# Memory branch, branch projections and second output projection as split products, memory handed over transposed

## The chip, the cores and the metric

One core of one Trainium2 chip runs the whole program in one launch. The metric is device time in microseconds (us). Three runs of the kernel before were timed; the number to be predicted is the median of the changed kernel. TensorE (PE in the profile, PEld its weight loads) multiplies matrices into PSUM, VectorE (DVE) and ScalarE (ACT) do elementwise work, GpSimd (POOL) and SyncE (SP) only start DMAs here. All arithmetic is in 32-bit floats.

## The reference

256 tokens of width 1024 pass through two layers of a first kind and then two of a second kind. Cut to what the change touches:

```python
def memory_branch(mq, mem, w_mem_kv):                 # mem: 256 x 1024
    mk, mv = jnp.split(mem @ w_mem_kv, 2, axis=-1)    # 512 wide each, 4 heads of 128
    p = softmax(q @ mk.T * 128 ** -0.5)
    return p @ mv

branches = (pool_branch(u_pool), dsa_branch(q, k, v, iq, ik, iw), memory_branch(mq, mem))
merged = sum(sigmoid(gate_logits[n]) * (branches[n] @ w_br[n]) for n in range(3))   # 512 -> 1024 each
x = layer_norm(DN_ALPHA * x + merged @ w_out)
x = layer_norm(DN_ALPHA * x + moe(x))                 # 16 experts, two per token
```

`pool_branch` takes sliding means, `dsa_branch` attends to 64 keys per query that an index score has picked. The second kind of layer has three attentions side by side (called swa, fox and mls in the kernel), whose results, 1024 wide, go through `w_out_2`; a feed-forward of width 4096 follows.

## The kernel before, in words

**Products.** `product` (from L540) has two forms. If both operands come in two parts, a rounded high part (type fp32r) and the rounded rest, it issues three rounded matmuls: high by rest, rest by high, high by high. Otherwise it issues one f32 matmul, which the profile shows as two instructions. The input projections, gates, `w_out` and the feed-forward were split already. The memory keys and values, the projections of the branches (`w_br`), the second output projection (`w_out_2`) and the experts were not.

**Weights.** Each weight piece is up to 1 MB (128 x 2048) and lies in a ring of 9 slots. A split piece takes two positions of the ring: SP loads the raw piece into the first as soon as that slot is released; ACT rounds it into the second (`round_hi`, L1127), once that slot is released too; then DVE subtracts in place (`round_lo`, L1469). An unsplit piece takes one position. SP loads strictly in the order of the plan (`weight_plan`). In each queue the calls `round_hi(n)` and `round_lo(n)` say at which point of that engine's own order all pieces up to number n are split. Nothing else sets when it happens: every engine works through its instructions in the order in which they are written, and waits on semaphores.

**The mixing layer.** Seven `cut`s make the columns z of the input projection (14 pieces, numbers 0 to 13). Between them stand the index scores, the pool branch and the transposition of the index queries, of memory (`pe_turn(("memT", l), mem_rows, ...)`) and of ik. After the last cut come the index scores of block 1, two key pieces (14, 15), the values (16, 17), two query pieces (18, 19), the transposition of the rotated Q and K, and the memory scores. In those same queues DVE finds the 64 best keys of each query (`top`) and rotates Q and K (`rope_heads`); ACT copies results out of PSUM.
Then follow 24 merges: for each of three branches (pool, memory, dsa) eight column groups `dc`. A merge is a gate product (8 chunks by 256 columns, split), a branch product (4 chunks, unsplit), ACT's sigmoid and DVE's multiplication. Each half of a branch (four merges) uses two gate pieces and one `w_br` piece, five positions of the ring. Between the merges of the first branch the two attentions are worked off: scores, exponentials, shares, transposed probabilities, values. `round_hi` and `round_lo` stand at every fourth merge and ask for the next three pieces; the product with `w_out` ("mixed") follows.

**Banks.** Four PSUM banks serve the large products in turn (`dense`), four the small ones (`loose`). A bank is free again when the engine that reads it has signalled; for the branch outputs that is ACT's copy.

**The second kind of layer.** Six cuts, then the three attentions in one long exchange between PE, ACT and DVE, then "attended" (the product with `w_out_2`, four pieces of 128 x 2048), then the feed-forward.

Of the kernel before, what the change touches and what calls it, by code (L numbers as in the profile page):

```python
# [9 lines left out]
ALU = mybir.AluOpType  # L10
# [3 lines left out]
P = 128  # L14
S = 256
# [102 lines left out]
class Signal:  # L118


    def __init__(self, sem, per_layer):
        self.sem, self.per_layer = sem, per_layer

    def at(self, l, i=0):
        return self.sem, l * self.per_layer + i + 1

    def last(self, l):
        return self.sem, (l + 1) * self.per_layer
# [114 lines left out]
def weight_plan(first_layers, second_layers):  # L243

    plan = []
    for l in range(first_layers):
        for cut in Z_CUTS:
            plan += [(w, True) for w in halves("w_in", (l,), (0, D), cut, "rows")]
        plan += [(w, False) for w in halves("w_mem_kv", (l,), (0, D), (0, BANK), "cols")]
        plan += [(w, False) for w in halves("w_mem_kv", (l,), (0, D), (BANK, 2 * BANK), "rows")]  # L250
        plan += [(w, True) for w in halves("w_in", (l,), (0, D), (C_MQ, C_GATE), "cols")]
        for n in BRANCH_ORDER:
            for a in (0, BANK):
                at = C_GATE + n * D + a
                plan += [(w, True) for w in halves("w_in", (l,), (0, D), (at, at + BANK), "cols")]
                plan.append((block("w_br", (l, n), (0, BRANCH), (a, a + BANK)), False))
# [40 lines left out]
def build_program(nc, t, out, first_layers=DEPTH, second_layers=DEPTH):  # L297
    with ExitStack() as ctx:
# [29 lines left out]
        mkT = sb("mkT", MEM_HEADS, N_MEM)  # L328
        mv = sb("mv", TB, BRANCH)
# [31 lines left out]
        mem_rows = shaped(region[:, TB * C_MQ + 4 * TB * 5 * HD:TB * C_MQ + 4 * TB * 5 * HD + TB * D], TB, D)  # L361
        memT = mergedT
        band = shaped(region[:, band_at:band_at + POOL_GROUPS * TB * S], POOL_GROUPS, TB, S)
# [27 lines left out]
        yT = part(KC, S)  # L391
        swa = dict(turned=part(TB, 10 * HD), probs=part(8, S), probsT=part(8, S), qT=part(4, S), kT=part(2, S))
# [71 lines left out]

        x_in, consts_in, params_in, router_in, positions_in, out_stored = (
# [3 lines left out]
        def landed(s, l, loads):  # L469
# [11 lines left out]
        memT_made, mk_made, mv_made, mq_made = (  # L481
            signal(n, c) for n, c in (("memT_made", 4), ("mk_made", 4), ("mv_made", 2), ("mq_made", 4)))
# [4 lines left out]
            signal(n, c) for n, c in (("dsa_scored", 16), ("dsa_lowered", 2), ("dsa_exped", 16), ("dsa_shared", 2),  # L487
                                      ("dsa_turned", 6), ("dsa_out", 8)))
        mem_scored, mem_lowered, mem_exped, mem_shared, mem_turned, mem_out = (
            signal(n, c) for n, c in (("mem_scored", 8), ("mem_lowered", 2), ("mem_exped", 8), ("mem_shared", 2),  # L490
                                      ("mem_turned", 4), ("mem_out", 8)))
# [15 lines left out]
            signal(n, c) for n, c in (("swa_scored", 16), ("swa_lowered", 2), ("swa_exped", 16), ("sink_exped", 2),  # L507
                                      ("swa_shared", 2), ("swa_turned", 6), ("swa_out", 8)))
# [6 lines left out]
            signal(n, c) for n, c in (("fox_scored", 8), ("fox_lowered", 2), ("fox_exped", 8), ("fox_shared", 2),  # L515
                                      ("fox_turned", 3), ("fox_out", 4)))
# [4 lines left out]
            signal(n, c) for n, c in (("mls_valued", 2), ("mls_summed", 2), ("mls_rooted", 2), ("mls_opened", 2), ("mls_y", 1)))  # L521
        relued, relu_squared, hidden_hi, hidden_lo = (
# [167 lines left out]
        def pe_pool(l, groups):  # L690
            for n in groups:
# [7 lines left out]
                i, free, full = loose.take(("pooled", l, n), pooled.at(l, n))  # L699
# [22 lines left out]
        def pe_mem_values(l, b):  # L722
            for h in range(MEM_HEADS):
                i, free, full = loose.take(("mem_out", l, b, h), mem_out.at(l, b * 4 + h))
# [12 lines left out]

        def pe_merge(l, m, dc):

            n, c = BRANCH_ORDER[m], dc % 4  # L740
            branch_ready = (pooled.last(l), mem_out.last(l), dsa_out.last(l))[m]
            if c == 0:
                held_pieces["gates"] = [ring.next() for _ in range(2)]
                held_pieces["projection"] = ring.next()
            gates, projection = held_pieces["gates"], held_pieces["projection"]
# [3 lines left out]
            pe_cols(("branch", l, m, dc), projection, c * P, [branchT[:, 4 * n:4 * n + 4, :]], weighed.at(l, m * 8 + dc),  # L749
# [4 lines left out]
        def tensor_mix(l):  # L754
# [5 lines left out]
            def key_piece(n):  # L760
                piece = ring.next()
                for j in range(2):
                    h = 2 * n + j
                    pe_cols(("mk", l, h), piece, j * P, [memT], mk_made.at(l, h), memT_made.last(l))
# [15 lines left out]
            pe_turn(("memT", l), mem_rows, D, [memT_made.at(l, n) for n in range(4)], landed(mem_in, l, 1))  # L780
# [9 lines left out]
            pe_index(l, 1, range(0, 4))  # L790
            key_piece(0)
            pe_index(l, 1, range(4, 8))
            key_piece(1)
            pe_rows(("mv", l), [memT], BRANCH, [mv_made.at(l, b) for b in range(TB)], memT_made.last(l))
            query_piece(0)
            query_piece(1)
# [15 lines left out]
                      [dsa_out.at(l, n) for n in range(4)], dsa_turned.at(l, 1))  # L812
# [1489 lines left out]
```

## Time and profile before

| | |
|---|---|
| three runs | 2008.25, 2011.35, 2012.51 us |
| median | 2011.35 us |
| the profiled execution | 2013.33 us |
| its span | 2011.8 us |
| TensorE busy | 1753.5 us (87%) in 9214 matmuls |
| VectorE busy | 774.0 us (38%) |
| ScalarE busy | 642.6 us (32%) |
| mean granted TensorE clock | 0.914 |
| weight traffic | 380.30 MB, 49.4% of 16 DMA engines |

The span is that of one execution taken by the profiler. A row of a timeline gives the start in us, the duration in us, the engine, the line of the kernel, the operation, what is written and read, how many instructions are merged into the row, and in brackets how long the engine had been idle and what it waited for. Most matmuls stand under L538, the helper that issues them, so they are told apart by their operands: `ring_rounded` is a split weight piece, `ring_sb` an unsplit one, `region_sb` the working area. A row with one granted clock is a row of the busy times by stretch.

### The profile page before, as it was taken

Reading aid. Unit: us, or ns where it says so; the run is one execution under the profiler, and the core shown is the slowest. Engines: PE = TensorE matmul, PEld = TensorE weight load, DVE = VectorE, ACT = ScalarE, POOL = GpSimd, SP = SyncE. Lnnn points to the kernel's source line nnn. Section 1 sums busy time; section 2 is a strip of 40 time slices with the busy share of each in tenths; the row PEclk is TensorE's granted clock in tenths of the full one; section 3 lists DMA queues with packets and bytes.
Section 4 is the critical chain, followed back from the end, with each engine's and each line's share of the span. In section 5 each row is a group of like instructions: output and inputs, shape, how many; then the busy total and the mean of one; then the engine's idle time right before and its main releaser. Section 6 shows DMA issues by size and latency. Waiting matters only on the chain.

```text
span 2011.8 us, 22089 instructions
## 1 busy us (share of the span) xinstructions
PE 1753.5 (87%) x9214; PEld 1288.5 (64%) x9214; DVE 774.0 (38%) x1476; ACT 642.6 (32%) x1041; POOL 29.5 (1%) x49
## 2 busy tenths in 40 slices
PE   6998986899997998986899995857899988588999
PEld 5777985444435777985444434844599977447997
DVE  4445343210115545333210015643455545515554
ACT  3326422010004336422011013443344444415442
POOL 4000000000000000000000000000000000000000
PEclk9998998799998998998899997965899998678999
DMA  8332345499995432335499992510255545003552
GB/s 258 138 126 93 147 147 219 176 401 421 421 420 178 153 125 89 147 147 218 173 414 421 421 421 99 197 40 0 84 189 188 178 142 183 1 21 126 189 189 105
DMA packets 57663, 392.67 MB, mean 195 GB/s; under 512 B 7124, under 2 KB 7168, under 8 KB 15696
## 3 DMA queue, kind: packets, MB, share of 16 engines
q1 hardware_dynamic: 54144, 380.30, 49.4%
q0 software_dynamic: 3264, 9.61, 1.4%
q8 instruction: 76, 1.25, 0.3%
q10 hardware_dynamic: 144, 1.24, 0.2%
q14 instruction: 35, 0.29, 0.0%
HBM read 390.07 MB, written 1.05 MB: 194 GB/s over the span
## 4 chain that ended last, share of the span: by engine, by line
PE 79%; DVE 10%; ACT 5%; DMA 4%; issue 2%; SPq 0%; DVEq 0%; ACTq 0%
PE psum L538 76%; DMA ring_sb<-in_weights 4%; PE psum L664 2%; ACT ring_rounded L1127 1%; DVE ring_rounded L1469 1%; PE psum L583 1%; ACT region_sb L1153 1%; DVE x_sb L1580 0%; ACT xT_hi_rounded L1352 0%; DVE x_sb L1578 0%; DVE region_sb L1853 0%; DVE region_sb L1856 0%; DVE small_sb L1849 0%; ACT region_sb L1341 0%; DVE region_sb L1847 0%
## 5 line engine op out<-in xcount | busy, mean ns | idle before, releaser
L538 PE MATMUL psum<-ring_sb,region_sb 128*64 128x512 f32 (+1 forms) x1728 | 427.0, 599 | 14.9 <-ACT region_sb L1341 11.0
L1469 DVE TENSOR_TENSOR ring_rounded<-ring_sb,ring_rounded 128x2048 fp32r<-128x2048 f32 (+4 forms) x152 | 321.5, 2130 | 245.6 <-ACT ring_rounded L1127 245.4
L538 PE MATMUL psum<-xT_hi_rounded,ring_rounded 128*128 128x256 f32 x1920 | 357.9, 288 | 0.0
L1127 ACT ACTIVATE ring_rounded<-ring_sb 128x2048 fp32r<-128x2048 f32 (+4 forms) x152 | 268.1, 1781 | 212.7 <-PE psum L538 149.9
L538 PEld LDWEIGHTS psum<-ring_sb,region_sb 128*64 128x64 f32 (+1 forms) x1728 | 148.2, 144 | 277.5 <-issue 260.1
L538 PE MATMUL psum<-ring_rounded,xT_hi_rounded 128*128 128x384 f32 (+4 forms) x960 | 278.3, 367 | 37.1 <-DVE ring_rounded L1469 18.1
L538 PE MATMUL psum<-xT_lo_rounded,ring_rounded 128*128 128x256 f32 x960 | 285.8, 298 | 27.9 <-DVE ring_rounded L1469 16.8
L538 PEld LDWEIGHTS psum<-xT_hi_rounded,ring_rounded 128*128 128x128 f32 x1920 | 308.3, 197 | 1.8 <-issue 0.5
L538 PEld LDWEIGHTS psum<-ring_rounded,xT_hi_rounded 128*128 128x128 f32 x960 | 184.4, 198 | 61.9 <-issue 39.4
L538 PEld LDWEIGHTS psum<-xT_lo_rounded,ring_rounded 128*128 128x128 f32 x960 | 189.7, 198 | 31.6 <-issue 18.1
L538 PE MATMUL psum<-ring_rounded,region_rounded 128*128 128x512 f32 x768 | 178.7, 392 | 3.0 <-DVE region_rounded L2055 3.0
L538 PE MATMUL psum<-ring_rounded,xT_lo_rounded 128*128 128x384 f32 (+4 forms) x480 | 173.9, 362 | 0.0
L538 PEld LDWEIGHTS psum<-ring_rounded,region_rounded 128*128 128x128 f32 x768 | 144.3, 189 | 33.0 <-DVE region_rounded L2055 3.4
L538 PE MATMUL psum<-region_sb 128*64 128x128 f32 (+4 forms) x608 | 128.2, 416 | 5.3 <-ACT region_sb L1147 4.5
L538 PE MATMUL psum<-region_sb,ring_sb 128*128 128x256 f32 x512 | 119.5, 380 | 0.0
L538 PEld LDWEIGHTS psum<-region_sb 64*128 64x128 f32 (+2 forms) x608 | 70.0, 187 | 57.7 <-issue 45.4
L538 PEld LDWEIGHTS psum<-region_sb,ring_sb 128*128 128x128 f32 x512 | 93.7, 190 | 12.0 <-issue 1.3
L538 PEld LDWEIGHTS psum<-ring_rounded,xT_lo_rounded 128*128 128x128 f32 x480 | 95.4, 199 | 6.3
L1803 DVE TENSOR_TENSOR region_sb<-region_sb,psum 128x512 f32<-128x512 f32 x16 | 11.0, 687 | 220.1 <-ACT region_sb L1334 220.1
L1334 ACT ACTIVATE region_sb<-psum 128x512 f32<-128x512 f32 x16 | 9.6, 597 | 216.5 <-PE psum L538 216.5
L1827 DVE TENSOR_SCALAR region_sb<-psum,slot_gate_sb 128x512 f32<-128x512 f32 x32 | 24.0, 751 | 122.9 <-PE psum L538 122.9
L583 PE MATMUL psum<-consts_sb,region_sb 128*128 128x128 f32 x148 | 28.2, 357 | 46.8 <-DVE region_sb L1856 24.9
(239 smaller groups left out, 1345.1 us busy)
## 6 DMA issues: line engine op xcount, KB each, us to landing
ring_sb<-in_weights SPq DMA_DIRECT2D x324, 1024.0 KB, 7.8
ring_sb<-in_weights SPq DMA_DIRECT2D x24, 768.0 KB, 4.3
ring_sb<-in_weights SPq DMA_DIRECT2D x8, 904.0 KB, 4.5
ring_sb<-in_weights SPq DMA_DIRECT2D x8, 900.0 KB, 4.6
ring_sb<-in_weights SPq DMA_DIRECT2D x8, 584.0 KB, 14.3
region_sb<-in_mem POOLq DMA_DIRECT2D x2, 1024.0 KB, 8.5
region_sb<-in_pool_band POOLq DMA_DIRECT2D x2, 1024.0 KB, 10.0
region_sb<-in_ln_g POOLq DMA_DIRECT2D x4, 512.0 KB, 4.3
```

What stands on the lines that cost most here:

```text
L538: return nc.tensor.matmul(dst, lhsT, rhs, start=first, stop=last, skip_group_check=True)
L583: last = nc.tensor.transpose(psum[:, i, j * S + b * P:j * S + (b + 1) * P], src[:, b, (c + j) * P:(c + j + 1) * P], ident)
L664: last = nc.tensor.transpose(psum[:, i, j * P:(j + 1) * P], scores[:, h, kb * P:(kb + 1) * P], ident)
L1127: nc.scalar.activation(rounded(piece.hi), piece.raw, ACT.Copy).then_inc(hi_made, 1)
L1153: nc.scalar.activation(scores[:, h, 0:keys], scores[:, h, 0:keys], ACT.Exp, bias=minus[:, h:h + 1], scale=scale, accum_out=sums[:, h:h + 1 ...
L1334: nc.scalar.activation(opened[pair % 2], psum[:, i, :], ACT.Sigmoid).then_inc(sig_made.sem, 1)
L1469: nc.vector.tensor_tensor(rounded(piece.raw), piece.raw, reread(piece.hi), ALU.subtract).then_inc(lo_made, 1)
L1803: nc.vector.tensor_tensor(rows, sig, psum[:, i, :], ALU.mult).then_inc(sig_read.sem, 1)
L1827: nc.vector.tensor_scalar(y[:, half * BANK:(half + 1) * BANK], psum[:, i, :], slot_gate[:, pair - 1:pair], None, ALU.mult).then_inc(gated. ...
```

## The change

- The two key and two value pieces, the six `w_br` pieces of a mixing layer and the four `w_out_2` pieces of a second layer are now split. Each takes two ring positions instead of one, and ACT and DVE each get 28 more splits in all (152 become 180).
- Their other operands are split too. ACT writes each branch output rounded, and DVE subtracts it from PSUM to make the rest; the bank is then free after DVE (`branch_lo`, `y_lo`), no longer after ACT. That is 20 small instructions per mixing layer and 13 per second layer.
- Memory comes transposed from the host (`mem_turned`), so its 16 transposes and their four copies per mixing layer go; ACT rounds it (128 x 2048) and DVE makes its rest.
- The query pieces now come before the key pieces: 14, 15 query, 16, 17 keys, 18, 19 values. Within a half of a branch the `w_br` piece comes between the two gate pieces. The calls of `round_hi` and `round_lo` are placed anew, in the merges at the second and fourth of four.
- Some semaphores are shared between the two kinds of layer.

```diff
 def weight_plan
-        plan += [(w, False) for w in halves("w_mem_kv", (l,), (0, D), (0, BANK), "cols")]
-        plan += [(w, False) for w in halves("w_mem_kv", (l,), (0, D), (BANK, 2 * BANK), "rows")]
         plan += [(w, True) for w in halves("w_in", (l,), (0, D), (C_MQ, C_GATE), "cols")]
+        plan += [(w, True) for w in halves("w_mem_kv", (l,), (0, D), (0, BANK), "cols")]
+        plan += [(w, True) for w in halves("w_mem_kv", (l,), (0, D), (BANK, 2 * BANK), "rows")]
-                plan += [(w, True) for w in halves("w_in", (l,), (0, D), (at, at + BANK), "cols")]
-                plan.append((block("w_br", (l, n), (0, BRANCH), (a, a + BANK)), False))
+                gates = halves("w_in", (l,), (0, D), (at, at + BANK), "cols")
+                plan += [(gates[0], True), (block("w_br", (l, n), (0, BRANCH), (a, a + BANK)), True), (gates[1], True)]
...
-            plan += [(w, False) for w in halves("w_out_2", (l,), (0, D), (a, a + BANK), "rows")]
+            plan += [(w, True) for w in halves("w_out_2", (l,), (0, D), (a, a + BANK), "rows")]
 TensorE, tensor_mix
-            pe_turn(("memT", l), mem_rows, D, [memT_made.at(l, n) for n in range(4)], landed(mem_in, l, 1))
...
             pe_index(l, 1, range(0, 4))
+            query_piece(0)
+            pe_index(l, 1, range(4, 8))
+            query_piece(1)
             key_piece(0)
-            pe_index(l, 1, range(4, 8))
             key_piece(1)
-            pe_rows(("mv", l), [memT], BRANCH, [mv_made.at(l, b) for b in range(TB)], memT_made.last(l))
-            query_piece(0)
-            query_piece(1)
+            pe_rows(("mv", l), [mem_hi, memT], BRANCH, [mv_made.at(l, b) for b in range(TB)], mem_split.at(l, 1))
 ScalarE, scalar_mix
             def merge(m, dc):
-                if dc % 4 == 0:
-                    round_hi(first + 20 + m * 6 + dc // 4 * 3 + 6)
+                if dc % 2:
+                    round_hi(first + 20 + m * 6 + dc // 4 * 3 + (4 if dc % 4 == 1 else 5))
...
             cut(6)
+            a.wait_ge(*landed(mem_in, l, 1))
+            nc.scalar.activation(rounded(mem_hi), memT, ACT.Copy).then_inc(mem_split.sem, 1)
             index(1, range(0, 4))
+            query_piece(0)
+            index(1, range(4, 8))
+            round_hi(first + 18)
+            query_piece(1)
             key_piece(0)
-            index(1, range(4, 8))
             key_piece(1)
-            round_hi(first + 20 + 2)
+            round_hi(first + 20)
             for b in range(TB):
...
                 nc.scalar.activation(mv[:, b, :], psum[:, i, :], ACT.Copy).then_inc(mv_made.sem, 1)
-            query_piece(0)
-            query_piece(1)
+            round_hi(first + 22)
 VectorE, vector_mix
+            def lower_mem(b):
+                for h in range(MEM_HEADS):
+                    i, _ = loose.of(("mem_out", l, b, h))
+                    v.wait_ge(*mem_out.at(l, b * 4 + h))
+                    nc.vector.tensor_tensor(rounded(z[:, b, C_IQ + h * P:C_IQ + (h + 1) * P]), psum[:, i, 0:P],
+                                            reread(branchT[:, 8 + h, b * P:(b + 1) * P]), ALU.subtract).then_inc(branch_lo.sem, 1)
...
             index(1, range(0, 4))
+            v.wait_ge(*mem_split.at(l, 0))
+            nc.vector.tensor_tensor(rounded(memT), memT, reread(mem_hi), ALU.subtract).then_inc(mem_split.sem, 1)
             index(1, range(4, 8))
-            round_lo(first + 20 + 2)
+            round_lo(first + 20)
             top(1, range(0, 8))
+            round_lo(first + 22)
...
             dsa_shares(0)
+            lower_mem(0)
             mem_scores(1)
...
             merge(0, 4)
+            lower_dsa(0)
             dsa_scores(1, range(0, 4))
             merge(0, 5)
             dsa_scores(1, range(4, 8))
+            lower_mem(1)
 ScalarE, scalar_second
             nc.scalar.activation(low, low, ACT.Ln, bias=const("one")).then_inc(decay_logged.sem, 1)
+            round_hi(first + 14)
...
+            round_hi(first + 16)
             act_mls_weights(l, 0)
 VectorE, vector_second
             swa_scores(1)
+            round_lo(first + 14)
+            lower_values("swa_out", swa_out, 0, 4, 0)
             mls_gates(0)
...
             fox_scores(1)
+            round_lo(first + 16)
             mls_out(1)
             fox_shares(1)
+            lower_values("fox_out", fox_out, 1, 2, 4)
...
+            nc.vector.tensor_tensor(rounded(y_lower[:, 6:8, :]), psum[:, i, :].rearrange("p (c t) -> p c t", c=2),
+                                    reread(yT[:, 6:8, :]), ALU.subtract).then_inc(y_lo.sem, 1)
```

## Rows read from the trace of the kernel before

**Rows 1.** Waits of PE: engine, line <- releaser: us in total, times, longest.

```profile
PE psum L538 <- DVE ring_rounded L1469: 34.9, 6, 8.4
PE psum L538 <- DVE xT_lo_rounded L1732: 16.1, 2, 8.1
PE psum L538 <- ACT upT_sb L1174: 11.0, 2, 5.5
```

**Rows 2.** Timeline of PE, two merges of the first layer.

```profile
215.83 1.89 PE L538 MATMUL psum<-region_sb,ring_sb 128*128 128x256 f32 x8
...
217.92 0.28 PE L538 MATMUL psum<-xT_lo_rounded,ring_rounded 128*128 128x256 f32 x1
...
220.43 1.89 PE L538 MATMUL psum<-region_sb,ring_sb 128*128 128x256 f32 x8
```

**Rows 3.** Values, "attended" (timeline) and "mixed" (chain, start and us).

```profile
128.21 13.90 PE L538 MATMUL psum<-ring_sb,region_sb 128*128 128x512 f32 x32
...
1398.18 30.14 PE L538 MATMUL psum<-ring_sb,region_sb 128*128 128x512 f32 x64 [0.78 <-ACT region_sb L1133]
...
315.56 24.61 PE psum L538 x96
```

**Rows 4.** Timeline from the last cut to the turned K, first layer.

```profile
111.97 1.13 PE L538 MATMUL psum<-region_sb 64*128 64x256 f32 x8
...
128.41 0.38 ACT L1220 ACTIVATE mkT_sb<-psum 128x256 f32<-128x256 f32 x1 [3.07 <-PE psum L538]
128.69 5.50 ACT L1127 ACTIVATE ring_rounded<-ring_sb 128x2048 fp32r<-128x2048 f32 x3
130.62 8.95 DVE L1469 TENSOR_TENSOR ring_rounded<-ring_sb,ring_rounded 128x2048 fp32r<-128x2048 f32 x4 [7.09 <-ACT ring_rounded L1127]
...
142.14 0.60 ACT L1273 ACTIVATE mv_sb<-psum 128x512 f32<-128x512 f32 x1 [2.84 <-PE psum L538]
...
147.78 0.42 DVE L1489 TENSOR_TENSOR region_sb<-region_sb,pos_cos_sb 128x256 f32<-128x256 f32 x1
...
151.73 0.42 DVE L1495 TENSOR_TENSOR region_sb<-region_sb 128x256 f32<-128x256 f32 x1
...
153.46 1.04 PE L583 MATMUL psum<-consts_sb,region_sb 128*128 128x128 f32 x8
159.07 1.97 PE L583 MATMUL psum<-consts_sb,region_sb 128*128 128x128 f32 x8 [4.58 <-DVE region_sb L1495]
```

**Rows 5.** By stretch: busy of PE, PEld, DVE, ACT, POOL; clock, DMA, GB/s.

```profile
159.00:163.90 4.90, 4.83 (x17) 4.20 (x17) 1.79 (x6) 3.42 (x4) 0.00 (x0) 0.50 0.00 0
...
178.50:181.00 2.50, 2.50 (x13) 2.50 (x12) 0.00 (x0) 2.48 (x7) 0.00 (x0) 0.50 0.30 128
...
296.00:301.00 5.00, 4.92 (x24) 4.93 (x25) 3.50 (x5) 0.39 (x2) 0.00 (x0) 0.54 0.00 0
```

**Rows 6.** Timeline of PE: ik is turned.

```profile
59.82 0.44 PE L583 MATMUL psum<-consts_sb,region_sb 128*128 128x128 f32 x2 [0.43 <-DVE region_sb L1683]
```

**Rows 7.** Timeline of PE between the merges of the first branch.

```profile
177.27 1.61 PE L664 MATMUL psum<-consts_sb,region_sb 128*128 128x128 f32 x8 [2.26 <-DVE region_sb L1508]
...
201.37 2.22 PE L538 MATMUL psum<-region_sb 64*128 64x256 f32 x8 [2.24 <-ACT region_sb L1147]
...
226.75 1.91 PE L664 MATMUL psum<-consts_sb,region_sb 128*128 128x128 f32 x16
```

**Rows 8.** Timeline, last half of the third branch and the output projection.

```profile
293.75 1.91 ACT L1127 ACTIVATE ring_rounded<-ring_sb 128x2048 fp32r<-128x2048 f32 x1 [7.30 <-DMA ring_sb<-in_weights]
296.08 0.58 PE L538 MATMUL psum<-xT_lo_rounded,ring_rounded 128*128 128x256 f32 x1 [5.55 <-ACT upT_sb L1174]
...
310.58 1.91 ACT L1127 ACTIVATE ring_rounded<-ring_sb 128x2048 fp32r<-128x2048 f32 x1 [4.29 <-DMA ring_sb<-in_weights]
```

**Rows 9.** Timeline, attentions of the first layer of the second kind.

```profile
1328.72 2.07 PE L538 MATMUL psum<-upT_sb,consts_sb 8*128 8x128 f32 x8 [4.29 <-ACT region_sb L1147]
...
1387.10 0.42 DVE L2000 TENSOR_TENSOR region_sb<-psum,small_sb 128x256 f32<-128x256 f32 x1 [4.32 <-PE psum L538]
```

More of the change, by code:

```diff
@@ L698, in pe_pool @@
                 last.then_inc(full, 1)
[L699 removed]
+                i, free, full = loose.take(("pooled", l, n), branch_lo.at(l, n))
                 pe.wait_ge(*differ_made.at(l, n))
@@ L736, in build_program, with z_columns @@
         held_pieces = {}
+        def z_columns(at):
+            return z[:, :, at:at + 4 * P].rearrange("p b (c t) -> p c b t", c=4)
+        lower_branch = {0: z_columns(C_POOL), 1: dsa_lo, 2: z_columns(C_IQ)}
         def pe_merge(l, m, dc):
             n, c = BRANCH_ORDER[m], dc % 4
-            branch_ready = (pooled.last(l), mem_out.last(l), dsa_out.last(l))[m]
+            branch_ready = branch_lo.at(l, (3, MEM_LO[1] + 3, DSA_LO[1] + 3)[m])
             if c == 0:
-                held_pieces["gates"] = [ring.next() for _ in range(2)]
+                held_pieces["gates"] = [ring.next()]
                 held_pieces["projection"] = ring.next()
+                held_pieces["gates"].append(ring.next())
             gates, projection = held_pieces["gates"], held_pieces["projection"]
@@ L1386, in cut @@
             def cut(n):
-                round_hi(first + 2 * n + 5)
+                round_hi(first + min(2 * n + 5, 2 * len(Z2_CUTS)))
                 c0, c1 = Z2_CUTS[n]
@@ L1659, in merge @@
             def merge(m, dc):
-                if dc % 4 == 0:
-                    round_lo(first + 20 + m * 6 + dc // 4 * 3 + 6)
+                if dc % 2:
+                    round_lo(first + 20 + m * 6 + dc // 4 * 3 + (4 if dc % 4 == 1 else 5))
                 vec_merge(l, m, dc)
@@ L1724, in vector_mix @@
             dsa_shares(1)
-            for dc in range(8):
+            merge(1, 0)
+            merge(1, 1)
+            lower_dsa(1)
+            for dc in range(2, 8):
                 merge(1, dc)
@@ L1902, in swa_shares, with lower_values @@
                 vec_shares("swa", b, swa["probs"], SWA_HEADS, (b + 1) * P, swa_shared)
+            def lower_values(name, out_made, b, pairs, row):
+                for pair in range(pairs):
+                    i, _ = loose.of((name, l, b, pair))
+                    v.wait_ge(*out_made.at(l, pairs * b + pair))
+                    nc.vector.tensor_tensor(rounded(y_lower[:, row + pair, b * P:(b + 1) * P]), psum[:, i, 0:P],
+                                            reread(yT[:, row + pair, b * P:(b + 1) * P]), ALU.subtract).then_inc(y_lo.sem, 1)
             def decays():
@@ L2014, in vector_second @@
             swa_heads()
-            round_lo(first + 2 * 4 + 5)
+            round_lo(first + 2 * len(Z2_CUTS))
             swa_scores(0)
-            round_lo(first + 2 * 5 + 5)
             swa_shares(0)
```

110 lines of the change are left out of this document (68 added, 42 removed).

## The prediction

> **What bounds the kernel now.** I read the page's busy shares and the chain of waits first: the chain that ended last is 79% TensorE (PE), nearly all of it matmuls, so an edit counts where it shortens the matmul stream or makes it wait. Then who kept PE waiting: the longest entry is PE waiting for VectorE's (DVE) weight splitting at L1469, 34.9 us in 6 waits; the sigmoid of a merge (L1174) and the split of the merged rows (L1732) follow [rows 1]. Then each stage in order of time, first mixing layer first. The second one repeats it 603 us later with the same waits, so I price one and double; the same for the two layers of the second kind. Of ScalarE (ACT) and DVE I look only at where they stand in their own order, since both take their instructions strictly one after another.
>
> **The product itself.** An unsplit product is two f32 instructions, a split one is three rounded ones. With 256 columns: from 217.92 to 220.43 lie seven split products, 0.36 us each; one merge (8 split, 4 unsplit) repeats after 220.43 - 215.83 = 4.60, which leaves 1.72 for the four unsplit, 0.43 each [rows 2]. With 512 columns: 16 unsplit products of values take 13.90, 0.87 each. The 32 split ones of "mixed" take 24.61 with a start at half clock, which cost 2.3 (below); without it 0.70 each [rows 3]. So 0.072 is saved on a 256-column product, 0.17 on a 512-column one. On TensorE alone, a mixing layer saves 96 x 0.072 = 6.9 in the 24 branch projections, 32 x 0.072 = 2.3 in the memory keys and 16 x 0.17 = 2.7 in the values.
>
> The Trainium skill (FP8 and Floating Point Precision, "TensorE Precision Notes") has a true FP32 product as four passes through the array. Three passes for four would save a quarter, 0.11 instead of 0.072; over the 256 products of 256 columns that is about 10 us more than I count. The trace's 0.36 against 0.43 is a sixth, and I go by it [rows 2].
>
> **A. From the last z cut to the turned K (the deciding term).** Today PE ends the cut at 111.97, goes through keys, values and queries without a gap until it turns Q at 153.46, waits 4.58 for the rotation of K, and turns K at 159.07: 47.1 us [rows 4]. DVE meanwhile splits four pieces (8.95 for 4), runs the top-64 search (139.6 to 147.8, 8.2), and rotates Q (147.78 to 152.15) [rows 4]; nothing here made PE wait except K.
> After the change, counted from the end of the cut: index 1.1, two query pieces and two key pieces 4 x 16 x 0.36 = 23.0, index 1.1: PE is through the keys at 25.2. Now ACT rounds the two value pieces only after it has copied the last key head (0.4), because round_hi(first + 20) stands there; hi 1.9, DVE's lo 2.3, hand-overs 0.2: PE may start the values at 30.0, a new wait of 4.8. The values last 16 x 0.70 + 2.3 for the slow start = 13.5, to 43.5. DVE's search (8.2) is behind the second lo (from 32.3) and hides under that. But round_lo(first + 22) comes before Q's rotation and needs ACT's round_hi(first + 22), which comes after the copies of the values (0.7): hi to 46.1, then two lo of 2.24 (the second hi is covered) to 50.6, rotation of Q 4.4 to 55.1. PE turns Q there, having waited 11.6; at half clock 1.97 instead of 1.04, then rotation of K 4.5 and hand-overs 0.2: K is turned at 61.8. Against 47.1 that is **+14.7**. Bounds: the two waits could not fall below what they are by in-order engines unless pieces are split earlier, so 12; 18 if a piece lands late.
> The half clock is read from the rows: after idle times of 4.58, 2.26 and 5.55 the granted clock was 0.50, 0.50 and 0.54 for the next 4.9, 2.5 and 5 us, the lower of the two levels (1.2 GHz of 2.4) [rows 5]. That cost about 2.4, 1.3 to 1.7 and 2.1 us; I take 2.3 after a long wait and 1.5 to 1.7 after one of 2 to 3 us.
>
> **B. Earlier in the layer.** Taking out the 16 transposes of memory gains nothing: ik must wait for DVE until 59.82 anyway, at present 0.43 [rows 6]. The wait becomes 2.3, and may be followed by the half clock: 0 to +1.7, I take +1.5. A query piece is now split ahead of the second half of DVE's search for block 0, and its hi slot is free only at mid cut: pool waits +0.4 (0 to 3, where it lands late). The split of memory, of the size of a weight piece (ACT 1.9, DVE 2.3 [rows 4]), hides under the first query piece.
>
> **C. Merges of the first branch.** The rounding that stood ahead of merge 0 moves into merge 1, where ACT does it after the memory exponentials: 2 x 1.9 on ACT and the second lo (2.2) then stand before DVE's merge, the scores and mem_shares. PE waits there already, 2.26 at 177.27, so all of the added delay counts: +3.1. Later the lowering of memory and attention outputs (16 of about 0.28 us on DVE) stands between copy and bank release: about 1.2 at memory scores. On the other side ACT no longer rounds two pieces at merge 4, and the wait of 2.24 at 201.37 mostly goes with its half clock [rows 7]. Step by step DVE then finishes dsa_shares(1) some 2 us before today's 226.75, but PE, with its shorter products, is there 2.6 earlier still and waits (half clock, 1.7): net -0.4. Bounds for this paragraph's 2.7: -3 (ACT and DVE keep up) to +7.
>
> **D. The other two branches.** 15 merges are covered by PE alone: DVE splits 3 pieces per half (6.9) and merges (3.4) in 17 us. -15 x 0.288 = -4.3. Ring: a half now takes 6 positions of 9 instead of 5. A gate piece asked for at the start of a half lands 4.9 later, or by an estimate 7.4 with a second one beside it, its lo is there after 10 to 12, and it is needed after 17: covered, with 5 us to spare.
>
> **E. Last half and output projection.** Today round_hi at merge 20 asks for three w_out pieces at once; the third one's slot is freed by the second gate of that same half. ACT waits 7.30 for its landing with the sigmoid behind it, and PE waits 5.55 and restarts slowly [rows 5, 8]. After the change that request is spread, and this goes: -5.55 - 2.05 = -7.6 (0 to -7.6). At the end the last w_out piece is asked for when the last projection ends, not one projection earlier, lands 4.9 after it, and ACT and DVE still have to split it: 9.9 instead of today's 8.1 of waiting [rows 1, 8]. +1.8.
>
> One mixing layer: 14.7 + 1.5 + 0.4 + 3.1 - 0.4 - 4.3 - 7.6 + 1.8 = **+9.2**; two, +18.4.
>
> **F. A layer of the second kind.** "attended" falls from 30.14 to the 24.6 of the same shape in "mixed" [rows 3]: -5.5. ACT now rounds two pieces (3.7) before the opening sigmoid and the copies of the probabilities, delaying the block 1 scores by 2.0; ACT's and DVE's work is otherwise one after another there, and lowering four outputs before the banks are free adds 0.7 (PE waits for that copy today, 4.29 [rows 9]): +2.7. The second pair of pieces (4.5 on DVE) falls into DVE's wait of 4.32 before mls_out [rows 9]: +0.2. The last lowering (128x512, 0.7) lies on the path: +0.7. Sum -1.9 (-5 to +4), two layers -3.8. The later ff pieces land during "attended"; the feed-forward is untouched, and so are the experts, which run on weight traffic from the moment the output projection frees the ring.
>
> **Sum.** +18.4 - 3.8 = +14.6. The profiled execution took 2013.33 (span 2011.8), so 2027.9 of it; the median of the three runs is 2011.35, 2 us lower, so **2026**.
>
> **Rivals.**
> 1. Only TensorE's arithmetic counts, since the splitting is hidden: per mixing layer -5.3 in A (41.9 to 36.6), -6.9, -7.6, +1.8, and -5.5 per second layer: 2 x -18.0 - 11 = -47, 1964. It needs the value and gate pieces split before PE has finished the keys. For it: ACT and DVE are only 32% and 38% busy. Against: the places of round_hi(first + 20) and (first + 22), behind the last key and the values. Half of it (early landings, quick ACT, my C overdone) would give 1995 to 2007. This is the side of faster; it decides once the two waits of A are under 6 us together (now 16.4).
> 2. Gain and loss cancel: A's second wait is 8 rather than 11.6 and C stays at zero: -9 us, 2010 to 2017.
> 3. The shallower ring binds in D: with 6 positions each half waits for a landing of 2 to 4 us, with half clock: 5 halves x 2 layers x 3 = +30, 2056. Against: the 5 us of room in D.
>
> **How the numbers follow.** Forecast as summed 0.65, rival 1 (whole or half) 0.15, rival 2 0.08, rival 3 0.12. The range holds the forecast's own bounds (A 12 to 18, C -3 to +7, B, F) and the near parts of the rivals: 2005 to 2045. A measurement of this kernel tells 0.2% (4 us) from no change: faster 0.15, same 0.08, slower 0.77.
>
> **What the changed profile would show.** PE with two new waits per mixing layer, about 5 us for L1469's successor before the values and about 12 before Q is turned (L583 waiting for L1495's successor); the wait on the sigmoid at merge 20 gone; rounded 128x256 products 0.36 apart in the branch projections; "attended" near 25 us; 180 splits instead of 152 on ACT and DVE. If the wait before Q is under 6 us, or DVE does the search after PE has started the values without a wait for the gate pieces, step A is wrong; if PE waits within merges 8 to 23, step D is.

## The result, and the profile after

The changed kernel takes 2033.4 us (median of 4 runs, 2029.5 to 2034.3), the kernel before on the same chip 2009.8 (4 runs): ratio 1.0113, 95% interval 1.0093 to 1.0134. It is slower by 1.1%, some 23 us. The profiled execution has a span of 2032.5 us, 20.7 more than before; PE is busy for 1726.2 us instead of 1753.5, DVE for 858.7 instead of 774.0, ACT for 693.1 instead of 642.6. So TensorE has 27 us less work and the kernel is slower: the time is in waits and in the lower clock behind them (mean granted clock 0.903 instead of 0.914).

The page after, busy times:

```profile
PE 1726.2 (85%) x9534; PEld 1306.9 (64%) x9534; DVE 858.7 (42%) x1572; ACT 693.1 (34%) x1063; POOL 29.0 (1%) x49
```

Waits of PE after (engine, line <- releaser: us in total, times, longest); L1487 is the splitting that was L1469 in [rows 1]:

```profile
PE psum L549 <- DVE ring_rounded L1487: 43.8, 8, 8.4
PE psum L594 <- DVE region_sb L1513: 31.6, 4, 11.3
PE psum L606 <- DVE x_sb L1598: 26.9, 6, 12.9
...
PE psum L549 <- DVE xT_lo_rounded L1784: 19.6, 2, 9.8
```

Splitting makes PE wait 8 times instead of 6 and 8.9 us longer; the rotation (L1513), which ahead of K had 4.58 in [rows 4], now has 31.6 in four waits. The sigmoid's 11.0 in [rows 1] is no longer in the list. The third line was not in the forecast.

The stage that decided, timelines of PE, ACT and DVE after, first layer; compare [rows 4]:

```profile
115.22 1.13 PE L549 MATMUL psum<-region_sb 64*128 64x256 f32 x8
...
140.65 0.38 ACT L1234 ACTIVATE memory_kv_sb<-psum 128x256 f32<-128x256 f32 x1 [2.44 <-PE psum L549]
140.93 3.70 ACT L1141 ACTIVATE ring_rounded<-ring_sb 128x2048 fp32r<-128x2048 f32 x2
142.87 4.49 DVE L1487 TENSOR_TENSOR ring_rounded<-ring_sb,ring_rounded 128x2048 fp32r<-128x2048 f32 x2 [14.58 <-ACT ring_rounded L1141]
145.31 14.24 PE L549 MATMUL psum<-ring_rounded,region_rounded 128*128 128x512 f32 x48 [4.69 <-DVE ring_rounded L1487]
...
160.08 3.70 ACT L1141 ACTIVATE ring_rounded<-ring_sb 128x2048 fp32r<-128x2048 f32 x2
162.01 4.49 DVE L1487 TENSOR_TENSOR ring_rounded<-ring_sb,ring_rounded 128x2048 fp32r<-128x2048 f32 x2 [6.55 <-ACT ring_rounded L1141]
170.83 1.97 PE L594 MATMUL psum<-consts_sb,region_sb 128*128 128x128 f32 x8 [11.28 <-DVE region_sb L1513]
177.30 1.97 PE L594 MATMUL psum<-consts_sb,region_sb 128*128 128x128 f32 x8 [4.51 <-DVE region_sb L1513]
```

Read it downwards: ACT copies the last key head and only then makes the hi (the rounded part) of the value pieces; DVE, which had been idle for 14.58, then makes the lo (the rest). PE starts the values after 4.69. The same happens again with the gate and branch pieces, with Q's rotation behind them on DVE: 11.28.

The stages, in us, measured from one landmark of PE's timeline to the next (x turned, index of block 1, K turned, memory probabilities turned, second attention probabilities turned, start of "mixed"):

| stretch (term of the forecast) | forecast | first mixing layer | second |
|---|---|---|---|
| to the last cut (B) | +1.9 | 100.8 to 102.6, +1.8 | 94.1 to 96.2, +2.1 |
| to K turned (A) | +14.7 | 47.1 to 62.1, +15.0 | 47.0 to 61.5, +14.4 |
| to memory probabilities (C, first part) | +3.1 | 18.2 to 21.0, +2.8 | 18.7 to 20.6, +1.9 |
| to attention probabilities of block 1 (C, rest) | -0.4 | 49.5 to 47.4, -2.1 | 49.4 to 47.2, -2.2 |
| to "mixed" (D and E) | -10.1 | 88.8 to 78.3, -10.5 | 89.1 to 78.3, -10.8 |
| sum | +9.2 | +7.0 | +5.4 |

Step B went as forecast also in its parts: PE waits 2.17 for ik (2.3 forecast), and in the 5.6 us behind that wait the granted clock is 0.75 and then 0.65, where it was 1.00 before the change.

Behind "mixed", up to the next x turned, the first mixing layer loses 5.4 more and the second 1.2. The layers of the second kind give -4.2 and +4.5 up to the x turned behind "attended", their feed-forwards -0.7 and +0.7; the landing of x at the start gives +1.5. Together that is the 20.7 of the two spans.

### The profile page after: what moved, and what is told of

Read it like the earlier page. It is cut to its first block, busy times and chain, and to the rows that moved or that the text cites. A ratio compares the mean times of both kernels' runs of the same rounds, so it can differ in the third digit from the quotient of the medians.

```text
span 2032.5 us, 22855 instructions
## 1 busy us (share of the span) xinstructions
PE 1726.2 (85%) x9534; PEld 1306.9 (64%) x9534; DVE 858.7 (42%) x1572; ACT 693.1 (34%) x1063; POOL 29.0 (1%) x49
## 4 chain that ended last, share of the span: by engine, by line
PE 76%; DVE 13%; ACT 6%; DMA 3%; issue 2%; SPq 0%; DVEq 0%; ACTq 0%
PE psum L549 72%; DVE ring_rounded L1487 4%; DMA ring_sb<-in_weights 3%; ACT ring_rounded L1141 2%; PE psum L675 1%; PE psum L594 1%; DVE region_sb L1526 0%; DVE x_sb L1598 0%; ACT xT_hi_rounded L1368 0%; DVE x_sb L1596 0%; DVE region_sb L1905 0%; ACT region_sb L1357 0%; DVE region_sb L1908 0%; DVE small_sb L1901 0%; DVE region_sb L1899 0%
## 5 line engine op out<-in xcount | busy, mean ns | idle before, releaser
L1487 DVE TENSOR_TENSOR ring_rounded<-ring_sb,ring_rounded 128x2048 fp32r<-128x2048 f32 (+4 forms) x180 | 384.8, 2156 | 271.2 <-ACT ring_rounded L1141 271.1
L1141 ACT ACTIVATE ring_rounded<-ring_sb 128x2048 fp32r<-128x2048 f32 (+4 forms) x180 | 320.5, 1801 | 185.9 <-PE psum L549 157.8
L549 PE MATMUL psum<-xT_hi_rounded,ring_rounded 128*128 128x256 f32 x1920 | 353.3, 286 | 0.0
L549 PE MATMUL psum<-ring_sb,region_sb 128*64 128x512 f32 x1536 | 340.9, 599 | 13.5 <-ACT region_sb L1357 11.0
L549 PE MATMUL psum<-xT_lo_rounded,ring_rounded 128*128 128x256 f32 x960 | 277.2, 289 | 16.8 <-DVE ring_rounded L1487 16.8
L549 PE MATMUL psum<-ring_rounded,region_rounded 128*128 128x512 f32 x992 | 249.4, 402 | 15.3 <-DVE ring_rounded L1487 9.4
L549 PEld LDWEIGHTS psum<-ring_sb,region_sb 128*64 128x64 f32 x1536 | 110.6, 138 | 229.6 <-issue 212.3
L549 PEld LDWEIGHTS psum<-ring_rounded,region_rounded 128*128 128x128 f32 x992 | 191.6, 195 | 57.9 <-issue 13.5
L549 PEld LDWEIGHTS psum<-region_sb 64*128 64x128 f32 (+2 forms) x608 | 72.2, 193 | 51.0 <-issue 41.5
L549 PE MATMUL psum<-region_rounded,ring_rounded 128*128 128x256 f32 x768 | 98.9, 280 | 0.0
L549 PEld LDWEIGHTS psum<-region_rounded,ring_rounded 128*128 128x128 f32 x768 | 94.4, 189 | 0.0
L594 PE MATMUL psum<-consts_sb,region_sb 128*128 128x128 f32 x116 | 27.4, 405 | 75.5 <-DVE region_sb L1513 31.6
```

The costliest lines, as they stand in the source:

```text
L549: return nc.tensor.matmul(dst, lhsT, rhs, start=first, stop=last, skip_group_check=True)
L594: last = nc.tensor.transpose(psum[:, i, j * S + b * P:j * S + (b + 1) * P], src[:, b, (c + j) * P:(c + j + 1) * P], ident)
L1141: nc.scalar.activation(rounded(piece.hi), piece.raw, ACT.Copy).then_inc(hi_made, 1)
L1487: nc.vector.tensor_tensor(rounded(piece.raw), piece.raw, reread(piece.hi), ALU.subtract).then_inc(lo_made, 1)
```

## The experiments

All ratios are of a kernel to the kernel before, with its 95% interval; kernels 1 to 4 shared one chip and its runs of the kernel before, 5 to 8 another, and 9, 10 and the second profile of kernel 4 a third. All stages are of the first layer unless said otherwise.

**1. Value pieces rounded early** (e1_values_early).

```diff
+            round_hi(first + 20)
             key_piece(0)
             key_piece(1)
-            round_hi(first + 20)
```

> The changed kernel (2033.4, 1.0113 of the kernel before) with one line of ACT moved: the hi of both value pieces stands ahead of the key heads' copies, not behind them. Theory (step A, the wait is made by ACT's order): the hi pieces are made while PE is in the key products, PE starts the values when the keys end, the wait of 4.9 us before the values goes and the half clock behind it (about 2 us) with it, while the wait of 11.3 before Q is turned stays, because the gate pieces are still rounded behind the copies of the values: 7 us per mixing layer, 2019, ratio 1.0045. Rival (the splitting engines have no time to spare there, so that the work is only moved): the second wait grows by what the first loses, 2031 to 2034. Rival (the pieces land late): no change, 2033.

Measured: 2020.1, ratio 1.0041 (1.0028 to 1.0054). Timeline of PE:

```profile
114.90 1.13 PE L549 MATMUL psum<-region_sb 64*128 64x256 f32 x8
...
140.14 11.36 PE L549 MATMUL psum<-ring_rounded,region_rounded 128*128 128x512 f32 x48
...
162.78 1.97 PE L594 MATMUL psum<-consts_sb,region_sb 128*128 128x128 f32 x8 [11.28 <-DVE region_sb L1513]
169.26 1.97 PE L594 MATMUL psum<-consts_sb,region_sb 128*128 128x128 f32 x8 [4.51 <-DVE region_sb L1513]
```

The wait before the values is gone, the 48 products take 11.36 instead of 14.24, and A falls to 54.4. The second wait is unchanged at 11.28: the work was not merely moved.

**2. Q rotated ahead of the lo of the gate pieces** (e2_rope_first).

```diff
-            round_lo(first + 22)
             rope_heads(C_Q, 0)
+            round_lo(first + 22)
```

> The changed kernel with one line of DVE moved: Q is rotated ahead of the lo of the first two pieces of the first branch, not behind them. Theory (step A, second wait is DVE's order and what ACT does ahead of it): Q is turned as the values end, about 10 us earlier; the two lo (4.5) and the rotation of K (4.5) then lie between the turning of Q and of K, so that the wait before K grows from 4.5 to about 9: 5 to 6 us per mixing layer, 2022, ratio 1.006. Rival (the copies of the values on ACT and the rounding behind them set the time, not DVE's order): less than 2 us per layer, 2030 to 2033.

Measured: 2019.9, ratio 1.0038 (1.0024 to 1.0052). Timeline of PE:

```profile
144.62 12.72 PE L549 MATMUL psum<-ring_rounded,region_rounded 128*128 128x512 f32 x48 [4.69 <-DVE ring_rounded L1487]
159.30 1.09 PE L594 MATMUL psum<-consts_sb,region_sb 128*128 128x128 f32 x8 [1.96 <-DVE region_sb L1513]
168.62 1.97 PE L594 MATMUL psum<-consts_sb,region_sb 128*128 128x128 f32 x8 [8.23 <-DVE region_sb L1513]
```

PE waits 1.96 before Q and 8.23 before K instead of 11.28 and 4.51, which is 5.6 less, as expected. A is 54.1, 8.0 less: Q is also turned at full clock (1.09 instead of 1.97 for eight), and the values happen to take 12.72 instead of 14.24 behind the same wait of 4.69. In the second layer A is 54.9, 6.5 less. The rival (under 2 us) is out.

**3. Both, with the gate and branch pieces rounded ahead of the values' copies as well** (e3_both_early).

```diff
             key_piece(1)
+            round_hi(first + 22)
...
                 nc.scalar.activation(mv[:, b, :], psum[:, i, :], ACT.Copy).then_inc(mv_made.sem, 1)
-            round_hi(first + 22)
```

> The changed kernel with three lines moved: value pieces' hi ahead of the key heads' copies, gate and branch pieces' hi ahead of the values' copies, and Q's rotation ahead of their lo. Theory (step A is order alone, the engines have the time): no wait before the values, Q turned within 2 us of their end, K 4.5 to 6 later; from the last cut to the turned K 45 us instead of 62.1, 16 to 17 per mixing layer, 2000 to 2002, ratio 0.995 to 0.996: faster than the kernel before. Rival (the delay comes back later, since DVE has 2 x 2.2 us more to do before the scores and merges of the first branch wait for it): only half is kept, 2015 to 2018.

Measured: 1991.8, ratio 0.9903 (0.9889 to 0.9917), faster than the kernel before. Timeline of PE:

```profile
114.10 1.13 PE L549 MATMUL psum<-region_sb 64*128 64x256 f32 x8
...
139.33 11.37 PE L549 MATMUL psum<-ring_rounded,region_rounded 128*128 128x512 f32 x48
150.54 1.03 PE L594 MATMUL psum<-consts_sb,region_sb 128*128 128x128 f32 x8
156.32 1.61 PE L594 MATMUL psum<-consts_sb,region_sb 128*128 128x128 f32 x8 [4.75 <-DVE region_sb L1513]
```

A is 42.2 in both layers instead of 62.1 and 61.5, that is 4.9 and 4.8 less than before the change. Index to Q turned is 36.4 against 41.5 in [rows 4]: -5.05, where the forecast had 5.3 for the arithmetic. The Trainium skill (FP8 and Floating Point Precision, "TensorE Precision Notes") has a true FP32 product as four passes through the array; three for four would save 6.9 here, an estimate: a quarter of 32 x 0.43 and 16 x 0.87. The trace does not agree. The whole gain arrives, and more than the expected 16 to 17 a layer.

**4. The second kind alone** (e4_second_only: in the kernel before, w_out_2 split and the attended rows lowered, that is split by DVE's subtraction, as in the change).

```diff
-            plan += [(w, False) for w in halves("w_out_2", (l,), (0, D), (a, a + BANK), "rows")]
+            plan += [(w, True) for w in halves("w_out_2", (l,), (0, D), (a, a + BANK), "rows")]
...
+            round_lo(first + 14)
+            lower_values("swa_out", swa_out, 0, 4, 0)
```

> The kernel before with only the second-kind layers' part of the change: w_out_2 split, the attended rows lowered; the mixing layers are as before. Theory (step F): 5.5 to 5.8 us less in each output projection, 2.7 to 4 given back by rounding in the middle of the attention and by lowering the last values: 2 per layer, 2006, ratio 0.998. The trace of the changed kernel had -4 in one such layer and +4.5 in the other, where one stretch ran at half clock that had run at full clock before. Rival (that half clock is brought about by the rounding): 2010 to 2015, ratio 1.000 to 1.003. Rival (the half clock came from where the stretch stood in time, nothing to do with the change): 2002 to 2004.

Measured: 2013.9, ratio 1.0015 (1.0006 to 1.0023): not the gain of 4 that the forecast had. One of twelve runs was far below the others, and it was the profiled one; hence a second profile:

> The kernel of e4_second_only once more, for a second profile: the first one was of the fastest of its twelve runs (2006.7, the others 2012.8 to 2016.5). Theory (the difference is TensorE's clock in the stretch of the second-kind attention between the turning of the second Q and the turning of the probabilities): there at least one layer shows 22 to 23 us at a granted clock of 0.50 to 0.57 where the first profile had 21 to 22, and the output projections are as before, 24 to 25 us. Rival (another stage varies): those stretches as in the first profile, the difference in the z cuts or the feed-forward.

The second profile is of a run of 2014.6. From the second Q turned to the probabilities turned the first profile has 22.8 and 21.1 us in the two layers, the second 21.3 and 22.8: the same sum, so that my reason for the difference between the two profiles fell. It is made of pieces of 1 to 2.5 us in the z cuts, around the feed-forward and in the mixing layers, at other granted clocks. But both have 44 in the two layers together, where the kernel before has 20.8 and 17.6: these 5.6 us are the larger part of the 6 between forecast and measurement.

**5. Branches alone** (e5_branches_only: the changed kernel with keys and values unsplit and ahead of the queries; w_out_2 stays split).

```diff
-            query_piece(1)
             key_piece(0)
             key_piece(1)
-            pe_rows(("mv", l), [mem_hi, memT], BRANCH, [mv_made.at(l, b) for b in range(TB)], mem_split.at(l, 1))
+            pe_rows(("mv", l), [memT], BRANCH, [mv_made.at(l, b) for b in range(TB)], landed(mem_in, l, 1))
+            query_piece(0)
+            query_piece(1)
```

> The changed kernel with the memory keys and values unsplit again and ahead of the queries, as in the kernel before (transposed memory, branch projections and w_out_2 stay split; no step A). Theory (A is the loss): by the measured length of A, 62.1 instead of 47.1 us per mixing layer, this kernel is 30 us under the changed one, 2003, ratio 0.996; by the forecast's own remaining terms 1996. Rival (the split of the branch projections with its extra roundings is what costs, A would have been won back elsewhere): 2011 or more.

Measured: 2003.9, ratio 0.995 (0.9934 to 0.9967). K is turned at 160.80, 47.0 after the index at 113.77, as in the kernel before. The time is the 2003 expected from A's measured length. Without step A the change gains 0.5%; with it, it loses 1.1%.

**6. The spread request alone** (e6_spread_request: in the kernel before).

```diff
-                if dc % 4 == 0:
+                if m == 2 and dc > 3:
+                    round_hi(first + {4: 38, 5: 39, 6: 39, 7: 40}[dc])
+                elif dc % 4 == 0:
                     round_hi(first + 20 + m * 6 + dc // 4 * 3 + 6)
```

DVE's queue has the same edit for `round_lo`.

> The kernel before with one edit: in the last half of the merges the three w_out pieces are rounded one after another (merges 20, 21 and 23) instead of all ahead of the sigmoid of merge 20. Theory (step E: ACT stood waiting for the third piece with the sigmoid behind it): PE's wait of 5.55 at merge 20 and the half clock behind it go, 7 to 7.6 per mixing layer, 1996 to 1998, ratio 0.993. Rival (the third piece is late all the same, and PE waits for it in the output projection): 2005 to 2011.

Measured: 1989.2, ratio 0.9881 (0.9861 to 0.9901). Timeline of ACT in the last half, and PE's start of "mixed"; compare [rows 8]:

```profile
282.93 1.90 ACT L1127 ACTIVATE ring_rounded<-ring_sb 128x2048 fp32r<-128x2048 f32 x1
...
292.12 1.90 ACT L1127 ACTIVATE ring_rounded<-ring_sb 128x2048 fp32r<-128x2048 f32 x1
...
296.71 1.90 ACT L1127 ACTIVATE ring_rounded<-ring_sb 128x2048 fp32r<-128x2048 f32 x1
301.51 1.91 ACT L1127 ACTIVATE ring_rounded<-ring_sb 128x2048 fp32r<-128x2048 f32 x1 [2.90 <-DMA ring_sb<-in_weights]
306.49 0.76 PE L538 MATMUL psum<-ring_rounded,xT_hi_rounded 128*128 128x512 f32 x1 [8.46 <-DVE xT_lo_rounded L1736]
```

ACT no longer waits 7.30 with the sigmoid behind it. From the wait of 2.24 in [rows 7] to "mixed" it is 106.6 instead of 114.2: 7.6 in the first layer, 9.4 in the second. The median fell by 24, more than these 17. The two profiled runs differ by 22.3; the 5 beyond the 17 lie in pieces of up to 1.4 us in stretches that the edit does not touch (the experts, the earlier parts of the mixing layers), and I can't assign them.

**7. The rounding ahead of merge 1 taken apart** (e7_merge_rounding: on kernel 3). ACT's `round_hi(first + 23)`, behind the copies of the values, is not shown; the condition of the merges changes in both queues.

```diff
             rope_heads(C_K, 1)
+            round_lo(first + 23)
             mem_scores(0)
...
-                if dc % 2:
+                if dc % 2 and m + dc > 1 or m == 0 and dc == 2:
```

> The kernel of e3_both_early with the rounding that stood ahead of merge 1 taken apart: the second gate piece of the first half is rounded behind the copies of the values and lowered behind K's rotation, where DVE waited 2.56 us; the first gate piece of the next half is rounded at merge 2. Theory (step C: two pieces at 1.9 and 2.2 us stand ahead of the merge, the scores and mem_shares while PE waits 5.7 for mem_probs, before the change 2.3): 3 to 5 us per mixing layer, 1982 to 1986. Rival (the wait for mem_probs is set by the softmax chain itself, whose wait grows back later as dsa_shares): under 1 us per layer, 1990.

Measured: 1986.5, ratio 0.9863 (0.9845 to 0.9882); kernel 3 had 0.9903 on another chip, so 8 us, or 5 by the medians. PE's wait for the memory probabilities is 2.25 instead of 5.73:

```profile
174.80 1.21 PE L675 MATMUL psum<-consts_sb,region_sb 128*128 128x128 f32 x8 [2.25 <-DVE region_sb L1527]
```

K turned to them takes 16.8 instead of 20.3, within the expected 3 to 5; in the second layer it is 18.1 instead of 20.0, a little less than that.

**8. All of it** (e8_all: on kernel 7: Q turned between last key and first value, and in the second kind the pieces rounded before the decays).

```diff
             key_piece(1)
+            pe_turn(("q", l), turned, 512, [qT_made.at(l, n) for n in range(2)], q_roped.at(l, 1))
             pe_rows(("mv", l), [mem_hi, memT], BRANCH, [mv_made.at(l, b) for b in range(TB)], mem_split.at(l, 1))
-            pe_turn(("q", l), turned, 512, [qT_made.at(l, n) for n in range(2)], q_roped.at(l, 1))
...
+            round_hi(first + 14)
             cut(5)
```

> The kernel of e7_merge_rounding with two more moves. Mixing: Q is turned between the last key and the first value, so that K's rotation lies beside the values (PE waited 4.75 there, then half clock). Second kind: the two w_out_2 pieces that were rounded behind the decays are rounded and lowered in the idle stretches before them (ACT idle 3.5, DVE 4.5). Theory: 5 per mixing layer and 2.3 per second-kind layer under e7, 14 to 15 us together, 1968 to 1972. Rival (the values start late, since the lo of their pieces now stands behind Q's rotation): a wait of 2 to 4 us before the values, half of the gain in the mixing layers gone: 1973 to 1976.

Measured: 1965.3, ratio 0.9773 (0.9748 to 0.9798), the best of all. Timeline of PE:

```profile
114.63 1.13 PE L549 MATMUL psum<-region_sb 64*128 64x256 f32 x8
...
140.32 1.09 PE L594 MATMUL psum<-consts_sb,region_sb 128*128 128x128 f32 x8 [0.30 <-DVE region_sb L1514]
142.62 11.44 PE L549 MATMUL psum<-ring_rounded,region_rounded 128*128 128x512 f32 x48 [1.20 <-DVE ring_rounded L1488]
153.90 1.03 PE L594 MATMUL psum<-consts_sb,region_sb 128*128 128x128 f32 x8
```

A is 39.3 us, 7.8 under the kernel before, with waits of 1.5 in all. The time is below the expected 1968 to 1972, but not for the expected reasons. A falls by 3.0 a layer against kernel 7, not 5. Most of the gain lies in the second kind: from the second Q turned to the probabilities turned it takes 17.4 and 17.5 us, where kernel 7 has 21.1 and 22.8. Kernel 9 has that placement by itself.

**9. The second kind with early rounding** (e9_second_early: on kernel 4).

```diff
+            round_hi(first + 14)
             cut(5)
...
             swa_shares(0)
+            round_lo(first + 14)
             decays()
```

> The kernel of e4_second_only with the two w_out_2 pieces that were rounded behind the decays rounded (ACT) and lowered (DVE) ahead of them, in stretches where ACT was idle for 3.5 and DVE for 4.5 us. Theory (the 2.3 to 2.6 us of wait that the change added there go, and with the wait shorter the stretch behind it runs at full clock, as in e8_all, where it took 17.4 instead of 21 to 23): 6 to 8 per layer under e4, 1999 to 2002, ratio 0.994 to 0.995. Rival (only the wait goes, the clock stays): 2009.

Measured: 2004.0, ratio 0.9949 (0.9933 to 0.9965). By stretches, with busy times and then the granted clock, kernel 4 first and then this one, second such layer:

```profile
1713.40:1727.90 14.50, 2.07 (x8) 1.77 (x8) 10.10 (x31) 7.40 (x12) 0.00 (x0) 0.50 0.00 1
1727.90:1749.00 21.10, 17.26 (x92) 13.97 (x92) 11.62 (x43) 9.18 (x23) 0.00 (x0) 0.66 0.00 1
```

```profile
1713.50:1728.00 14.50, 2.07 (x8) 1.78 (x8) 10.11 (x31) 7.47 (x13) 0.00 (x0) 0.50 0.00 1
1728.00:1745.40 17.40, 13.59 (x92) 10.90 (x92) 11.51 (x43) 8.98 (x23) 0.00 (x0) 0.79 0.00 0
```

The same 92 instructions, 21.1 us at 0.66 and 17.4 at 0.79. The two layers have 20.7 and 17.4, as the kernel before with 20.8 and 17.6. The stretch ahead of each, 14.5 us at half clock with PE busy for 2.07, is alike in both kernels. What differs is the stretch before that one, from which the rounding was taken: 14.5 and 14.3 us instead of 16.7 and 16.6. That the placement brings the lower clock is shown (the eight profiles with the rounding late have 43.9 to 44.1 for the two layers, the two with it early 38.1 and 34.8); how, isn't.

**10. Thirty-one tiny DVE copies per mixing layer** (e10_padded: in the kernel before).

```diff
                 merge(2, dc)
+                for k in range(4 if dc else 3):
+                    nc.vector.tensor_copy(stat("pad", 62)[:, 31 * l + 4 * dc + k - (dc > 0):31 * l + 4 * dc + k + 1 - (dc > 0)], const("one"))
```

> The kernel before with 31 tiny DVE copies (128x1) in the merges of the third branch of each mixing layer, as many as the change adds instructions to DVE per mixing layer; DVE is idle there. Theory (the 5 us of DVE issue time at the end of the first experts come from where DVE's instructions lie, not from the work): DVE shows 5 us of issue ahead of its first addition behind the experts, PE's wait before it turns x grows from 7.8 to 12.6 us, 2016, ratio 1.0025. Rival (it comes from the change's data movement or its later loads): wait 7.8, no change, 2011.

Measured: 2015.1, ratio 1.0015 (1.0004 to 1.0026). After the experts of the first layer, timelines of DVE and PE, first of this kernel, then of the changed one:

```profile
617.87 0.69 DVE L1563 SCALAR_TENSOR_TENSOR x_sb<-x_sb,psum 128x512 f32<-128x512 f32 x1 [5.29 <-issue]
628.12 1.97 PE L595 MATMUL psum<-consts_sb,x_sb 128*128 128x128 f32 x8 [12.71 <-DVE x_sb L1580]
```

```profile
624.58 0.69 DVE L1581 SCALAR_TENSOR_TENSOR x_sb<-x_sb,psum 128x512 f32<-128x512 f32 x1 [5.46 <-issue]
634.84 1.97 PE L606 MATMUL psum<-consts_sb,x_sb 128*128 128x128 f32 x8 [12.88 <-DVE x_sb L1598]
```

PE waited 7.83 there before the change, and 7.84 in kernels 4, 6 and 9, which leave the number of DVE's instructions in the mixing layers as it was. Copies that compute nothing bring the 5 us. The whole kernel is slower by 0.15% where 0.25% was expected, which the interval just includes.

## Why the prediction was right

The forecast was 2026 and the time 2033. Sign and deciding step hold; the change was forecast at 14.6 and is 23.6 by the medians, 20.7 by the profiled spans. That the sum comes so near is in part luck: the mixing layers came 6.0 below the forecast, and the 6.6 behind them, which it did not have, made up for that. What remains is the second kind (4) and the start (1.5).

- **A**: +15.0 and +14.4 against +14.7, with waits of 4.69 and 11.28 against 4.8 and 11.6. Kernel 1 takes away the first wait (-7.7 in the stage), kernel 2 shortens the second (-8.0), kernel 3 does both (-19.9). The cause is the order of ACT's and DVE's instructions, not their load. Rival 1 named its own point of decision, the two new waits under 6 us together: kernel 3 has neither (its 4.75 is K's wait, 4.58 before the change) and is faster than the kernel before.
- **B**: +1.8 and +2.1 against +1.9, with the wait and the lower clock that were forecast.
- **C**: +2.8 and +1.9 against +3.1, and kernel 7 takes 3.5 of it back by moving the rounding. The rest was -2.1 instead of -0.4: the wait forecast before the attention probabilities of block 1 isn't there, and they are turned at full clock; waits of 0.80 and 2.38 earlier in the stretch (208.24 and 230.89) cost less. C as a whole is +0.7 and -0.3, not +2.7; kernel 7 shows the first part of it, and nothing tests the second.
- **D and E**: -10.5 and -10.8 against -10.1. "mixed" waits 9.82, forecast 9.9. Kernel 6 has E alone at 7.6 in the first layer. Rival 3 needed waits inside merges 8 to 23; PE shows none of 1 us or more there.
- **F failed in its sum**: -3.8 for the two layers, +0.3 in the profiled run, and +3 (1.0015) in kernel 4. Its terms held: "attended" fell from 30.14 in [rows 3] to 24.4, +2.3 and +2.6 for the rounding against +2.7, +0.7 for the last lowering. What was missing is the granted clock some 15 us behind that rounding, 5.6 us in the two layers: F's sum has no term for the clock at all.
- **Missing altogether**: the 5 us of DVE issue time behind the first experts (kernel 10). "The experts are untouched" was true of their work and not of the time at their end.
- **Slips in the working**: rival 1 takes A's arithmetic from 41.9 to 36.6, while [rows 4] give 41.5 from the index to Q turned; the 5.0 of its own products (2.3 and 2.7) is what kernel 3 shows (5.05). Rival 2's "-9 us" is 2 x (3.6 + 2.7) = 12.6 by its own conditions. Neither touches the forecast.

Rival 1's times came with other placements (kernel 3 at 1992, kernel 8 at 1965), rival 2's 2010 to 2017 with none of them: the same arithmetic ran from 1965 to 2033 by where a few instructions stood, nearly all of them roundings.

## What to carry to other kernels

When an operand becomes split in two parts, PE's saving is the small part of the sum. Walk each preparing instruction to its place in its engine's order and ask what stands ahead of it: here two lines on ACT and one on DVE were worth 42 us, nearly twice what the change lost. In this kernel it paid to place a preparing step as soon as its slot was free, ahead of copies that wait for PE. A request that waits for several loads at once should not stand ahead of something PE needs: kernel 6 gained 17 us that way, and 1.2% in all, in the kernel before the change. And do such a change in parts: without keys and values it gains 0.5%, the second kind alone 0.5% once its rounding stands early, while keys and values as placed cost 1.6%.

## What the runs showed of the hardware

- Five microseconds appear at the end of the first layer's experts, as issue time on DVE, when DVE has 31 more instructions ahead of them: the splits and subtractions of the change (5.46), or copies that compute nothing (5.29); the 26 more of kernel 5 bring it too (5.25). Before the change ACT had 5.00 of it there at 607.45, and DVE had none; behind the second layer's experts DVE had 4.91 of it already in the kernel before, at 1217.83. That it depends on which instructions lie ahead and not on their work is shown; what the engine does in that time isn't.
- A short idle does not always bring the lower clock: after waits of 2.26 the eight transposes of the memory probabilities took 1.61 in [rows 7], 1.94 in kernel 6, 1.21 in kernel 7 and 1.09 (full clock) in kernel 8 after 2.25.
- The kernel before itself ranged from 2006.1 to 2017.5 over the runs of three chips, with mean granted clocks of 0.914 to 0.919 on the first, the longer ones at the lower: ratios of 1.0015 came clear of 1 only with twelve and ten runs (kernels 4 and 10), against 17 and more of the kernel before.
